# Gated recurrence: levels 5 and 6 of the decayed attention computed only for the keys that are read, as 32 by 32 and 64 by 64 products

## The reference, cut to what matters

```python
def hgrn2_recurrence(q, k, v, logf):        # 16 heads, head width 128, 256 tokens
    # S_t = diag(f_t) S_{t-1} + k_t v_t^T,  o_t = S_t^T q_t
    b = jnp.cumsum(logf, axis=-2)
    decay = jnp.exp(jnp.where(incl, b[..., :, None, :] - b[..., None, :, :], -jnp.inf))
    attn = jnp.einsum("bhtd,bhsd,bhtsd->bhts", q_i, k_i, decay)
    o_i = q·exp(b) @ state + attn @ v_i
...
def hgrn2_mixer(x, w_in, lower_bound, hgrn_norm_g, w_out):
    q_raw, f_raw, i_in, z = jnp.split(x @ w_in, 4, axis=-1)
    f = lower_bound + (1.0 - lower_bound) * sigmoid(f_raw)
    q, k, logf = silu(q_raw), 1.0 - f, log(f)
    o = rms_norm(hgrn2_recurrence(q, k, i_in, logf), g) * silu(z)
    return o @ w_out
```

## Time and profile before

| | us |
|---|---|
| median of three runs | 1410.13 |
| lowest and highest | 1408.59, 1410.61 |
| the profiled execution | 1410.44 |
| its span, from first to last instruction | 1408.3 |

### The profile page before, as it was taken

The page is one execution under the profiler, slowest core; times in us unless marked ns, Lnnn a source line. Parts: engine busy times, 40 slices in busy tenths (PEclk is TensorE's granted clock), DMA queues, the critical chain, the costliest instruction groups (busy, mean ns, idle before and its releaser), DMA issues.

```text
span 1408.3 us, 24667 instructions
## 1 busy us (share of the span) xinstructions
PE 1348.1 (96%) x10464; PEld 1248.9 (89%) x10464; DVE 975.4 (69%) x1491; ACT 747.4 (53%) x989; POOL 22.4 (2%) x53
## 2 busy tenths in 40 slices
PE   6998998999989999999799998899999999999998
PEld 5997998999979999999798776888888998988887
DVE  4887977765466788777644686788776676576543
ACT  6666344437454455555245413778634686487531
POOL 0000000000000000000000000000000000000000
PEclk9998999999999999999899999999999999999999
DMA  6555553444266555555232323568875433355551
GB/s 254 184 194 191 183 215 133 188 168 147 98 224 225 182 202 190 205 209 181 91 120 90 121 91 122 180 222 288 300 269 206 150 120 121 131 185 194 190 195 64
DMA packets 34637, 247.22 MB, mean 176 GB/s; under 512 B 3872, under 2 KB 3872, under 8 KB 4960
## 3 DMA queue, kind: packets, MB, share of 16 engines
q1 hardware_dynamic: 29968, 213.40, 42.2%
q0 software_dynamic: 4560, 32.25, 6.5%
HBM read 244.58 MB, written 1.05 MB: 174 GB/s over the span
## 4 chain that ended last, share of the span: by engine, by line
PE 82%; DVE 8%; ACT 6%; issue 3%; DMA 1%; DVEq 0%; ACTq 0%
PE PS L467 14%; PE PS L409 9%; PE PS L410 9%; PE PS L411 9%; PE PS L468 7%; PE PS L482 6%; PE PS L865 3%; ACT WH L542 3%; DVE WL L555 2%; PE PS L425 2%; PE PS L929 2%; PE PS L426 2%; PE PS L427 2%; PE PS L742 1%; PE PS L730 1%
## 5 line engine op out<-in xcount | busy, mean ns | idle before, releaser
L555 DVE TENSOR_TENSOR WL<-RAW,WH 128x2048 fp32r<-128x2048 f32 x166 | 380.0, 2289 | 118.3 <-ACT WH L542 115.0
L542 ACT ACTIVATE WH<-RAW 128x2048 fp32r<-128x2048 f32 x166 | 317.0, 1910 | 182.2 <-PE PS L468 71.2
L409 PE MATMUL PS<-XW,WH 128*128 128x256 f32 x1024 | 301.1, 294 | 16.8 <-DVE WL L555 12.4
L410 PE MATMUL PS<-XW,WH 128*128 128x256 f32 x1024 | 293.2, 286 | 0.0
L411 PE MATMUL PS<-XW,WL 128*128 128x256 f32 x1024 | 292.9, 286 | 0.0
L409 PEld LDWEIGHTS PS<-XW,WH 128*128 128x128 f32 x1024 | 200.0, 195 | 18.4 <-DVE WL L555 12.4
L410 PEld LDWEIGHTS PS<-XW,WH 128*128 128x128 f32 x1024 | 200.1, 195 | 0.2
L411 PEld LDWEIGHTS PS<-XW,WL 128*128 128x128 f32 x1024 | 199.8, 195 | 0.0
L467 PE MATMUL PS<-XW,WH 128*128 128x512 f32 x392 | 141.0, 398 | 0.2
L296 DVE SCALAR_TENSOR_TENSOR BIG<-BIG,C 128x256 f32<-128x256 f32 (+2 forms) x228 | 101.4, 505 | 30.0 <-ACT BIG L1264 13.5
L468 PE MATMUL PS<-XW,WL 128*128 128x256 f32 x392 | 109.9, 280 | 0.0
(11 more groups left out here) (368 smaller groups left out, 2677.4 us busy)
## 6 DMA issues: line engine op xcount, KB each, us to landing
RAW<-wst SPq DMA_DIRECT2D x200, 1024.0 KB, 4.9
BIG<-wad POOLq DMA_DIRECT2D x30, 1024.0 KB, 5.1
X<-xT SPq DMA_DIRECT2D x1, 1024.0 KB, 4.9
outT<-X SPq DMA_DIRECT2D x4, 256.0 KB, 4.2
K<-cst SPq DMA_DIRECT2D x1, 656.0 KB
CB<-crow SPq DMA_DIRECT2D x1, 512.0 KB
BIG<-pT POOLq DMA_DIRECT2D x2, 256.0 KB, 4.2
C<-cols SPq DMA_DIRECT2D x1, 370.0 KB
```

The source lines that it names most:

```text
L409: pe.matmul(o, h, hl[0][:, k0 + k, :], start=(k == 0), stop=False)
L410: pe.matmul(o, h, hl[1][:, k0 + k, :], start=False, stop=False)
L542: ac.activation(WH[p % NS][:, :], RAW[u % NR][:, :], ACT.Copy).then_inc(S.hi.tick(p), 1)
L555: ve.tensor_tensor(WL[p % NS][:, :], RAW[u % NR][:, :], WH[p % NS][:, :].bitcast(f32), ALU.subtract).then_inc(S.lo.tick(p), 1)
```

## The change

In `pe_level`, levels 5 and 6 get branches of their own. At level 5 each of the four matmuls (128 keys by 64 queries) becomes two of 32 keys by 32 queries, for the blocks at tokens 0 and 64 of the half. Their outputs go to partitions 0 to 31 and 64 to 95, the same places as before. At level 6 each matmul takes 64 keys by 64 queries and writes partitions 0 to 63. What the copies read is the same numbers at the same places; the rest of the bank is no longer written. The contraction is over 128 channels as before. No instruction moves: on TensorE level 5 of a pair is eight matmuls in place of four at the same place in the order, level 6 four in place of four; the other engines, the semaphores and the DMAs are unchanged.

```diff
@@ -859,7 +859,16 @@
             else:
                 pe.wait_ge(*S.hg.ve("uq", hp, lv))
             vacate(pe, b, "lv", hp, lv)
-            if 0 <= lv < 7:
+            if lv == 5:
+                for m in range(4):
+                    for a in (0, 64):
+                        ks, qs = k[:, m // 2, 128 * (m % 2) + a:128 * (m % 2) + a + 32], q[:, m // 2, 128 * (m % 2) + a + 32:128 * (m % 2) + a + 64]
+                        t = pe.matmul(PS[b][a:a + 32, 64 * m + a // 2:64 * m + a // 2 + 32], ks, qs, start=True, stop=True)
+            elif lv == 6:
+                for m in range(4):
+                    c = 128 * (m % 2)
+                    t = pe.matmul(PS[b][0:64, 64 * m:64 * m + 64], k[:, m // 2, c:c + 64], q[:, m // 2, c + 64:c + 128], start=True, stop=True)
+            elif 0 <= lv < 7:
                 qs = by_blocks(q, 1 << lv)
                 for m in range(4):
                     t = pe.matmul(PS[b][:, m * 64:(m + 1) * 64], k[:, m // 2, blk(m % 2)], qs[:, m, :, 1, :], start=True, stop=True)
```

## The result

| | before | after |
|---|---|---|
| median | 1409.36 us (4 runs, 1407.55 to 1410.61) | 1402.34 us (4 runs, 1399.11 to 1402.96) |
| the profiled execution, its span | 1408.3 us | 1400.1 us |

The ratio is 0.9939, with a 95% interval of 0.9922 to 0.9956: the change makes the kernel faster by 7.0 us by the medians and 8.6 by the ratio (6.2 to 11.0). The forecast was 2.7 us, 1407.4, with a range down to 1405.0.

What follows compares the result with a forecast made beforehand. TensorE was taken to bound the kernel. Seven head pairs at 0.29 us (2.0) plus 0.8 in the last gave 2.8, taken as 2.7: 1410.13 - 2.7 = 1407.4 us, range for 8 in 10 1405.0 to 1410.4.

Steps and rivals of the forecast that it cites:

- What bounds the kernel: Recurrence, 438.10 to 668.80 us: TensorE busy throughout, so shortening its groups there shortens the path one for one.
- The switch of form: Entering and leaving the new matmul forms between projections: first start 0.21 us behind, not 0.12; 0.10 more on leaving.
- The third rival: Switching form costs nothing, so each head pair saves 0.85 us: 1403.4 us; chance 0.07.
- Level 6: Four 64 by 64 products between projections: 1.02 us in place of 1.13, saving 0.11 us in each of seven pairs.
- Level 5: Sixteen passes of 32 by 32 products between projections: 0.95 us in place of 1.13, saving 0.18 us per pair.
- the taps' 0.0235 us: Convolution's taps, 141 passes of 32 by 32 in 3.32 us: the nearest row used to price level 5's passes.
- the tap sum: Convolution's sum, eight passes in 0.57 us, 0.071 each; not used for level 5's price because it streams 256 columns.
- The last pair by its waits: Last head pair, priced to VectorE's release: level 5 saves 0.34 us, level 6 0.45, together 0.8.
- Only TensorE's instructions change: Whole kernel: no wait, DMA, evacuation or semaphore is added or moved; no cost was given to it.
- Slow small passes: Rival: load and matmul pairs far above 0.024 us (level 5 break-even 0.036): 3.7 us slower, 1413.9; chance 0.09.
- Given back: Rival: a wait between the levels takes the 2 us, leaving the last pair's 0.8: 1409.3 us; chance 0.08.
- The end's clock: Rival: a half-clock stretch in the last head pair moves, at most 3.05 us either way: 1410.4 or 1404.4; chance 0.12.

Runs made afterwards that it cites:

- e5: Kernel before with 32 tiny matmuls (128 TensorE instructions) added at the idle start: 3.2 us faster than before (1.3 to 5.2).
- e6: Changed kernel with 32 tiny matmuls added at the start, 256 TensorE instructions more than before in all: 5.2 us faster than before (3.0 to 7.3).
- e8: Changed kernel measured once more, nothing added: 7.1 us faster than before (4.2 to 9.7).
- e7: Kernel before with 64 tiny matmuls (256 TensorE instructions) added at the start: -1.3 us faster than before (-3.4 to 0.8).
- e15: Kernel before with 12 matmuls filling TensorE's idle times in the last head pair and 52 tiny ones at the start: 5.6 us faster (3.9 to 7.2).
- e16: Changed kernel with 32 tiny matmuls at the start, the program of e6 measured again: 3.9 us faster than before (1.4 to 6.6).

## Why the prediction was wrong, point by point

**What bounds the kernel**: right. TensorE stays busy through the seven pairs, and each level's time came off the span.

**The switch of form** (entry 0.09 over a plain step, exit 0.10): right to the hundredth in both new forms. The third rival, that it costs nothing, fell; that its number, 1403.4, lies nearest to the measured time is luck.

**Level 6**: 0.11 us forecast, 0.09 measured. **Level 5**: the term was mis-sized, 0.18 forecast and 0.32 measured. The step that failed was taking the taps' 0.0235 us as the fastest that pairs can follow. They follow at 0.017 in this form: 0.25 us from the first start to the last, where 0.39 was forecast (0.36 and the 0.03 of an open load). The taps stream 256 columns like the tap sum, which the prediction had set aside for just that, while level 5 streams 32. Seven pairs: 2.0 forecast, 2.8 measured.

**The last pair by its waits**: right where the clock is the same. In the changed kernel level 6 starts at 699.21 and VectorE goes on at 699.92, 0.71 us, where 0.69 was forecast and the earlier trace rows have 1.14. Level 5 takes 0.74, from the projection matmul at 697.65 to VectorE at 698.39, where 0.82 was forecast:

```profile
697.65 0.28 PE L411 MATMUL PS<-YW,WL 128*128 128x256 f32 x1
697.90 0.45 PE L866 MATMUL PS<-BIG 128*32 128x32 f32 x16
...
699.21 0.68 PE L870 MATMUL PS<-BIG 128*64 128x64 f32 x8 [0.86 <-DVE BIG L2065]
...
698.39 0.43 DVE L2064 TENSOR_TENSOR BIG<-BIG 128x256 f32<-128x256 f32 x1
...
699.92 0.42 DVE L2064 TENSOR_TENSOR BIG<-BIG 128x256 f32<-128x256 f32 x1 [0.69 <-PE PS L870]
```

**"Only TensorE's instructions change: no wait, DMA, evacuation or semaphore is added or moved."** This is the step that failed. The sentence is true of the program and was used as if the number of instructions were free. Level 5 has twice as many, 128 more over the kernel, and they moved every fetch behind them. The page of before had the sign: 3% of the chain under "issue", and the chain's list has the two stalls (most of the 3% lies elsewhere; these two are 5.3 us). They should have been a rival, with 5.3 us and the half clock behind the first, 1.7, as what it could bring.

**The rivals.** Slow small passes: fell, 0.017 against a break-even of 0.036. Given back: fell, the 2.8 us are in the span. The end's clock: it moved, in the direction to which I gave half of 0.12, and in the profiled pair by up to 5.5 us (6.3 us in the two stages less the 0.8 of the levels). I had bounded it by one stretch (3.05); there are three that can go.

**The size, put together** from the experiments rather than from one pair of profiles: 3.6 us are the levels' own rows, 2 to 3 the fetches (e5, e6 against e8), and what is left of the 7.0 to 8.6, 0.2 to 3 us, fits the clock in the last pair, but is no larger than the intervals.

The Trainium skill has a rule on the fetches. Runtime: NRT & Kernel Launch, section Instruction fetch mechanics, states that TensorE's instructions are refilled in blocks of 16 KiB, 256 instructions, and that the cost of crossing a boundary is mostly hidden. The first part agrees with the packets of 16384 bytes and the period of 256 (e7). The second doesn't hold everywhere here: at an edge in or just behind a dense burst of taps (141 passes in 3.32 us) TensorE can stand for up to 3.4 us (e15, e16), though not at every such edge, while those in the streams of projections leave no stall of TensorE.

## What to carry to other kernels

Count the instructions that an edit adds or removes on TensorE, and look in the chain of waits for "issue" on TensorE with an instruction packet beside it: wherever a dense burst of small matmuls stands further down, an edit anywhere ahead can move a stall of 2 to 3 us into it or out of it, and a control with the same number of idle instructions tells that from the edit's own worth. Where TensorE idles repeatedly behind other engines (here for 0.85 to 2.7 us), price the half clock with it: filling such idle time with needless matmuls won more here than the change itself did by its rows. Measure the speed of a new form of small matmul in its own form; the neighbouring form was 40% slower. And test a shift by several amounts: it took no single value, and its worth and that of the levels did not add up.

## What the runs showed of the hardware that was not expected

- Pairs of weight load and matmul with 32 weight columns, 32 moving columns and 128 rows, alternating between two output places (partitions 0 to 31 and 64 to 95), follow at 0.017 us on average; the 32 by 32 taps with 256 moving columns at 0.0235.
- Thirty-two tiny matmuls in idle time at the start make the kernel before 3.2 us faster (1.3 to 5.2), forty-eight 6.2 us (4.5 to 8.0), sixty-four not at all.
- Twelve needless matmuls of 0.21 us a pass in the idle times of the last pair make the old kernel 5.6 us faster (3.9 to 7.2), by keeping the granted clock at 1.00 from 680 to 710 us where it was 0.77 and 0.50.
- TensorE's 24 unexplained stops of over 0.5 us in 18 profiles all come at one and the same place in a block of 256 of its instructions, beside a fetch of 16384 bytes, and end 1.2 to 1.6 us behind it.
